# Every second weight slab of the later gates and branch products: its remainder made by an accumulating DMA

## The reference, cut to what matters

```
proj = h @ w_in                       # ... the last 6144 columns are the gates
y_a = (dsa_attention(...) * silu(za)) @ w_a_out
y_b = (conformer_conv(...) * silu(zb)) @ w_b_out
y_c = (stick_breaking_attention(...) * silu(zc)) @ w_c_out
g = sigmoid(gates).reshape(b, s, 3, 2048)
merged = g[:, :, 0] * y_a + g[:, :, 1] * y_b + g[:, :, 2] * y_c
return x + merged @ w_out
```

## Time and profile before

| | |
|---|---|
| median of three runs | 3022.87 us |
| the profiled execution: span from first to last instruction | 3020.0 us |
| PE busy | 3003.1 us (99%) |
| ACT busy | 2288.5 us (76%) |
| DVE busy | 2115.0 us (70%) |
| POOL busy | 7.7 us (0%) |
| transfers of the loads' queue, share of the 16 DMA engines | 61.0% |

### The profile page before, as it was taken

The page is one execution under the profiler, slowest core; times in us unless marked ns, Lnnn a source line. Parts: engine busy times, 40 slices in busy tenths (PEclk is TensorE's granted clock), DMA queues, the critical chain, the costliest instruction groups (busy, mean ns, idle before and its releaser), DMA issues.

```text
span 3020.0 us, 37810 instructions
## 1 busy us (share of the span) xinstructions
PE 3003.1 (99%) x13856; PEld 2510.0 (83%) x13856; DVE 2115.0 (70%) x3153; ACT 2288.5 (76%) x4062; POOL 7.7 (0%) x20
## 2 busy tenths in 40 slices
PE   8999999999999999999999999999999999999998
PEld 7888888878888888888888888888888888888887
DVE  6566656767666799999765555658999977555555
ACT  8799988999998677698984446786669999644564
POOL 0000000000000000000000000000000000000000
PEclk9999999999999999999999999999999999999999
DMA  8665665666556665566666666566566656666665
GB/s 307 198 175 167 180 201 174 203 181 178 178 175 199 190 192 176 172 181 181 188 184 194 190 194 196 190 198 192 162 195 180 177 172 196 187 208 192 193 191 165
DMA packets 305801, 570.24 MB, mean 189 GB/s; under 512 B 18352, under 2 KB 45136, under 8 KB 305232
## 3 DMA queue, kind: packets, MB, share of 16 engines
q1 hardware_dynamic: 301728, 557.65, 61.0%
q10 hardware_dynamic: 3040, 6.42, 0.6%
q0 software_dynamic: 848, 3.76, 0.4%
HBM read 565.66 MB, written 2.10 MB: 188 GB/s over the span
## 4 chain that ended last, share of the span: by engine, by line
PE 96%; ACT 3%; issue 0%; DMA 0%; DVE 0%; DVEq 0%; SPq 0%; ACTq 0%
PE gp L113 92%; PE bk L113 4%; ACT G L128 2%; ACT wh L128 1%; PE bk L116 0%; DMA raw<-in_ev_w_mem_kv 0%; ACT tmp L128 0%; ACT nat L128 0%; ACT Yh L128 0%; DVE wl L139 0%; DVE merged L152 0%; DVE X L139 0%; DVE merged L145 0%; DVE gp L146 0%; DVEq L2464 0%
## 5 line engine op out<-in xcount | busy, mean ns | idle before, releaser
L139 DVE TENSOR_TENSOR wl<-raw,wh 128x1024 fp32r<-128x1024 f32 (+2 forms) x1072 | 1281.3, 1201 | 723.7 <-ACT wh L128 719.8
L128 ACT ACTIVATE wh<-raw 128x1024 fp32r<-128x1024 f32 (+2 forms) x1072 | 1111.1, 1044 | 579.7 <-PE gp L113 557.9
L113 PE MATMUL gp<-wh,Hh 128*128 128x512 f32 (+2 forms) x2336 | 905.3, 388 | 0.0
L113 PE MATMUL gp<-wl,Hh 128*128 128x512 f32 (+2 forms) x2336 | 898.3, 385 | 0.0
L113 PE MATMUL gp<-wh,Hl 128*128 128x512 f32 (+2 forms) x2336 | 898.3, 385 | 0.0
L113 PE MATMUL gp<-wh,Yh 128*128 128x512 f32 (+3 forms) x1952 | 758.4, 389 | 8.8 <-DVE wl L139 8.8
L113 PE MATMUL gp<-wh,Yl 128*128 128x512 f32 (+3 forms) x1952 | 753.5, 386 | 0.0
L113 PE MATMUL gp<-wl,Yh 128*128 128x512 f32 (+3 forms) x1952 | 753.4, 386 | 0.0
L113 PEld LDWEIGHTS gp<-wh,Hh 128*128 128x128 f32 x2336 | 438.8, 188 | 87.7 <-issue 2.3
L113 PEld LDWEIGHTS gp<-wh,Hl 128*128 128x128 f32 x2336 | 438.7, 188 | 86.7
L113 PEld LDWEIGHTS gp<-wl,Hh 128*128 128x128 f32 x2336 | 438.9, 188 | 84.9
(11 more groups left out here) (135 smaller groups left out, 1196.7 us busy)
## 6 DMA issues: line engine op xcount, KB each, us to landing
raw<-in_w_in SPq DMA_DIRECT2D x544, 512.0 KB, 3.8
raw<-in_ev_w_in SPq DMA_DIRECT2D x104, 512.0 KB, 3.8
raw<-in_od_w_in SPq DMA_DIRECT2D x80, 512.0 KB, 3.7
raw<-in_w_out SPq DMA_DIRECT2D x64, 512.0 KB, 4.2
raw<-in_ev_w_out SPq DMA_DIRECT2D x40, 512.0 KB, 4.3
raw<-in_od_w_out SPq DMA_DIRECT2D x36, 512.0 KB, 4.0
raw<-in_w_b_out SPq DMA_DIRECT2D x32, 512.0 KB, 4.7
raw<-in_w_a_out SPq DMA_DIRECT2D x32, 512.0 KB, 4.9
```

What stands on the lines that cost most here:

```text
L113: return self.e.matmul(out, l, r, start=start, stop=stop)
L128: return self.e.activation(out, in_, func, **kw)
L139: return self.sketch(157 + size(a) * 1.042) if self.e is None else self.e.tensor_tensor(out, a, b, op)
```

## The change

The gates and branch products of branches 0 and 2 (the later two of the three) in layers 2 and 3 have 192 slabs. Of these, those with odd j, 96 slabs, get their remainder in another way. ACT first writes the negated rounding, -raw in the type fp32r, into wl, then wh as before. POOL then issues a DMA that adds raw onto wl, so that wl is raw - round(raw). DVE does nothing for these slabs. The wait of `mm(f)` and of the load `raw(f+4)` is now for this DMA to have landed (`s_rest`) in place of `lo(f)`.

More of the change, by code:

```diff
@@ L1004, in pad @@
         e.memset(P.glu[:, :, 0:30], 0.0).then_inc(*P.g_pad.up(l))
+    def rest(f):
+        gm, j = P.fills[f]
+        e.wait_ge(*P.a_hi.at(f))
+        e.dma_add(P.wl[f % SPLIT][:, :, 0:gm.n], P.raw[f % RAW][:, :, 0:gm.n]).then_inc(*P.s_rest[f % SPLIT].up(f, 16))
     return {"zero": zero, "clear_halves": clear_halves, "load_dil": load_dil, "load_constants": load_constants, "load_gfin": load_gfin, "load_second": load_second,
-            "load_cc": load_cc, "pad": pad}
+            "load_cc": load_cc, "pad": pad, "rest": rest}
 def pe_program(P, e):
```

## The result

The changed kernel takes 3140.44 us (median of four runs, 3135.95 to 3151.3) against 3022.89: ratio 1.0396, 95% interval 1.0379 to 1.0412. It is slower by 117 us; 3183 was forecast, in a range of 3020 to 3435. The profiled execution took 3137.32 us with a span of 3135.5, 115.5 more than before.

The account below looks back on a forecast made before the run. PE, busy 99% of the span, was taken as the bound, with no gain possible; a raw-buffer round of 2.2 + 7.0 + 5.0 = 14.2 us, 3.3 over PE's, times 48 gave about 160: 3020.0 + 160 + 2.87 = 3183 us, range 3020 to 3435.

Parts of the forecast that it names:

- Nothing to gain: In the two changed stretches PE is always busy; the 118 us taken off DVE lie off the path, gain 0 us.
- The loop through the raw buffer: Passes, add and next load on one raw buffer: 14.2 us a round against PE's 10.88, about 160 us over 48.
- R: Time of the next load into raw from issue to landing, taken as 5.0 us, ends 4.5 and 6.5.
- the loop through wl: Second loop at an added slab: 2.2 + L + 2.72 us, called shorter as long as R is over 2.72.
- L: Time of the adding DMA from issue to landing, taken as 7.0 us, ends 5.1 and 10.3.
- The wait on PE: PE would wait for the DMA onto wl, about 160 us in some 96 pieces.
- The Trainium skill on the landing: A GpSimd transfer takes 2.0 us plus bytes over 436 GB/s: 4.4 us for 1.05 MB, 3.2 for 512 KB.
- The Trainium skill on the add: In the adding DMA the sum is free; reading two sources costs, at half a copy's rate, so 1024 KB rows apply.
- Rival 1: The add is hidden behind PE, landing in under 4.2 us; no change, 3023 us, chance 0.12.
- Rival 2: The add is much slower than a load of the same bytes, 14.0 us to landing; 3590 us, chance 0.14.
- Rival 3: Waits before every second slab bring PE to the lower clock for good; 461 us more, 3484 us, chance 0.04.
- short slow starts: Some seven slow PE matmuls after a wait would cost 1.4 us and hide, since R exceeds a slab of 2.72 + 1.4.

Follow-up runs that it names:

- othersrc: Changed kernel with the adds reading tile X in place of raw, and the load of raw no longer waiting for them: 3142.93 us.
- Copy: Changed kernel with the 96 adds made plain copies of raw onto wl, which also drops the conversion to fp32r: 3083.09 us.
- same48: Changed kernel with 48 adds in place of 96, all in the same raw buffer (f mod 4 = 1): 3033.11 us.
- apart48: Changed kernel with 48 adds in place of 96, at slabs with f mod 8 = 1 or 3: 3091.93 us.
- sideload: Remainders from DVE as before the change; beside each of 96 slabs POOL issues a 512 KB add from X onto the output's memory: 3025.44 us.
- smalls: Changed kernel with each 512 KB add replaced by two 8 KB adds in sequence, the slab waiting for the second: 3141.65 us.

## Why the prediction came out as it did

- *Nothing to gain.* Right. PE waited for no DVE before, and negonly, which adds ACT's pass and leaves the rest, is at 3022.3.
- *The loop through the raw buffer.* Shown by the chain as what bounds most of the changed kernel's two stretches: 2.3 + 5.4 + R = 13.3 leaves R at 5.6, which is what the loads measure. It was right as a mechanism, but it is not the only limit, and in this the prediction was incomplete. It had the second one twice, as wl wanted 8.16 us after `hi`'s start and as the loop through wl of 2.2 + L + 2.72, and set it aside as shorter. It is shorter for a round of mean length, but a single add of 8 us is late for PE all the same, and there the chain of the changed kernel goes through PE. Open the loop through raw (othersrc) and the one through wl takes over at the same cost, with L up from a median of 5.0 to 7.5. That L grows because the loads that were held back now go out just ahead of the adds is a reading that fits the sorting by recent loads above; no run isolates it.
- *The wait on PE.* Forecast as some 160 us in some 96 pieces, it is 81.2 us in 50; the rest of the loss stands in PE's busy time. One wait a round follows from the prediction's own sentence that the loss is that of one loop.
- *L.* Taken as 7.0, measured 5.4 on the mean (4.4 at best). *R.* Taken as 5.0, measured 5.6 in the loop. The sum of both was 12.0 and is 11.0, so the round was put at 14.2 for 13.3: 48 x 0.9 = 43 us too much, the whole difference between 3183 and 3140. The mis-sized term is L, 1.6 us too long. R was 0.6 too short and the handovers 0.1, and that the errors partly cancel is luck: with L right and the rest as taken the forecast would have been 3106. The range of 3020 to 3435 was wide enough to hold either. The 1024 KB row was the wrong nearest row; between the 384 KB row and that one the truth lay at the lower end.
- *The Trainium skill on the landing* (DMA: Bandwidth & Descriptors, Anatomy of one DMA — SWDGE (gpsimd) path). The estimate from its 2.0 us plus bytes over 436 GB/s, with both operands counted, is 4.4 us, and the quickest adds take 4.4. The same estimate for a copy of 512 KB is 3.2 us, and the quickest here took 2.8, so there the measurement is below the page's formula. No add of 512 KB in these runs had no load at all beside it, so what one takes quite alone is not shown. The time that decided was that of the adds that met loads.
- *The Trainium skill on the add* (Collectives: The Full Stack, The bandwidth ceiling: the fold count and why AG ≠ RS ≠ AR) puts the price of a sum, in a ReduceScatter between cores, into its second read. Copy and changed kernel fit this, 4.6% against 9.1% of the engines for the queue with its 96 transfers of the same size; the landing, 2.8 against 4.4 us at best, is not doubled. They do not show it, since the copy drops the conversion as well. The prediction took from it that the 1024 KB rows are the right ones, and they were not.
- *Rival 1* (hidden) needed L under 4.2; no add got there, and same48 shows how near it was: with one add in four slabs the cost is 10 us.
- *Rival 2* (a slow add) is out: 4.4 us at best.
- *Rival 3* (the clock). In part. Stretches at a lower clock do occur where PE has waited, as in this window of 10 us:

```profile
1790.00:1800.00 10.00, 7.22 (x25) 5.67 (x25) 2.23 (x3) 3.67 (x5) 0.84 (x1) 0.83 0.85 201
```

The mean clock of 0.96 and 0.98 over 325 and 340 us is some 20 us of PE's time, and part of the 34.8 us that its busy time grew. The prediction said that short slow starts hide, since the load of a round is longer than a slab. Where the chain has no PE in it they do. But eight times in the two stretches the chain goes through 36 matmuls behind an add. Once they take 8.47 us:

```profile
1819.36 8.47 PE gp L113 x36
```

The other seven times they take 9.8 to 10.1, as the piece from 1654.59 on above, and in each the granted clock falls:

```profile
1654.30:1657.70 3.40, 3.11 (x7) 2.49 (x8) 0.40 (x1) 0.00 (x0) 0.00 (x0) 0.50 1.02 244
```

That is the level of 1.2 GHz. Seven times 1.3 to 1.6 us are 11 of the 115 us that the change costs, which the prediction had put at nothing; they stand inside the mean round of 13.3. No run was made without them.

## What to carry to other kernels

Work moved from an engine that nobody waits for to a transfer is paid in waiting more than in bytes: write down the rounds of each buffer and the lead of the consumer before and after, and ask of each whether a landing, at its stretched length, still fits. A transfer in such a round does not have one length; here the same add took 4.4 us at best and 7.2 us on the mean just behind loads (apart48), and where the trace was followed back those loads had been released by the landing of the add before. So the distance between such transfers matters beside their number: the same 48 cost 69, 31 or 10 us. With 64 of them at a distance of 3 the cost was 115, and what these runs show does not forecast that. When opening one limit changes nothing, look for the second one that the freed traffic has just reached.

## What was not expected of the hardware

- The DMA engines went to a share of 1.04 and 287 GB/s in sideload without slowing PE, while smalls, at 0.56 (before 0.65), lost 119 us. The share alone said nothing about the cost.
- An add of 8 KB took 2.0 us from issue to landing alone and up to 5.8 beside loads; one of 512 KB 4.4 at best and up to 8.8 in the changed kernel. The extra is about 4 us at both sizes.
- An add issued from GpSimd keeps it for 0.84 us, where its plain loads took 0.54 and the plain copies of the same tiles in copy 0.53.
